# Head norms by products with ones and roots on every partition, and a block inverse kept in one orientation

## What is computed

```
qkv_a = causal_dwconv_silu(pad_front(qkv_a), conv_w)
qa = l2_norm(qa.reshape(B_, Lp, H_A, DK_A)) * (DK_A ** -0.5)
ka = l2_norm(ka.reshape(B_, Lp, H_A, DK_A))
o_a = gated_delta_rule(qa, ka, va, beta, g)[:, PAD:]
o_a = rms_norm_2(o_a, o_norm_a) * jax.nn.silu(z_a.reshape(B_, L, H_A, DV_A))
qb = rms_norm_2(qb.reshape(B_, L, H_B, DH_B), q_norm_b)
kb = rms_norm_2(kb.reshape(B_, L, H_B, DH_B), k_norm_b)
o_b = forgetting_attention(pad_front(qb), pad_front(kb), pad_front(vb), pad_front(log_f))[:, PAD:]
gate = jax.nn.sigmoid(gates.reshape(B_, L, 2, D_MODEL))
return jnp.sum(gate * y, axis=2) @ w_out
```

## Time and profile before

| | us |
|---|---|
| median of 3 runs | 1982.2 |
| lowest and highest run | 1977.0, 1984.1 |
| profiled execution, its time | 1981.22 |
| profiled execution, its span | 1979.9 |

### The profile page before, as it was taken

One profiled execution on the slowest core, in us unless ns is written; L12 is line 12 of the kernel. 1 busy time (PEld: TensorE's weight loads), 2 busy tenths in 40 slices (PEclk: granted clock), 3 DMA queues, 4 the chain that ended last, 5 costly groups with the idle time before them and its releaser, 6 DMA issues. The chain is left out here.

```text
span 1979.9 us, 23713 instructions
## 1 busy us (share of the span) xinstructions
PE 1785.5 (90%) x9424; PEld 1353.9 (68%) x9424; DVE 1232.4 (62%) x2155; ACT 718.6 (36%) x1243; POOL 434.1 (22%) x373
## 2 busy tenths in 40 slices
PE   7989999999999999998989999997878787887878
PEld 6869988977799879888979777893333333333333
DVE  4766655665576557654464445688776677667754
ACT  3545534344355346642342344343221122212211
POOL 0330000310000000004022000033555545454541
PEclk9989999999999999989989979998889988888889
DMA  6334555444445543412221211479999999999995
GB/s 261 110 114 149 191 183 180 170 153 166 165 176 190 182 177 110 149 64 80 92 68 62 86 62 67 170 287 421 422 421 421 422 422 421 422 422 421 421 422 245
DMA packets 62621, 453.76 MB, mean 229 GB/s; under 512 B 6944, under 2 KB 7072, under 8 KB 7856
## 3 DMA queue, kind: packets, MB, share of 16 engines
q0 software_dynamic: 36864, 268.45, 32.6%
q1 hardware_dynamic: 25040, 178.27, 25.4%
q10 hardware_dynamic: 608, 5.53, 0.7%
HBM read 451.18 MB, written 1.05 MB: 228 GB/s over the span
## 5 line engine op out<-in xcount | busy, mean ns | idle before, releaser
L2346 PE MATMUL banks<-uv_rows,diag 128*128 128x512 f32 x1024 | 509.8, 662 | 126.9 <-ACT diag L2395 122.5
L553 DVE TENSOR_TENSOR weights_lo<-weights,weights_hi 128x1024 fp32r<-128x1024 f32 x336 | 422.7, 1299 | 284.9 <-ACT weights_hi L544 282.3
L2346 PEld LDWEIGHTS banks<-uv_rows,diag 128*128 128x128 f32 x1024 | 215.4, 214 | 420.6 <-issue 269.3
L544 ACT ACTIVATE weights_hi<-weights 128x1024 fp32r<-128x1024 f32 x336 | 336.7, 1051 | 388.5 <-PE banks L560 380.2
L558 PE MATMUL banks<-x_hi,weights_hi 128*128 128x256 f32 (+1 forms) x1472 | 428.6, 291 | 6.7 <-DVE weights_lo L553 3.6
L560 PE MATMUL banks<-x_hi,weights_lo 128*128 128x256 f32 (+1 forms) x1472 | 422.0, 287 | 0.0
L559 PE MATMUL banks<-x_lo,weights_hi 128*128 128x256 f32 (+1 forms) x1472 | 421.8, 287 | 0.0
L2482 DVE CUSTOM_DVE_ANT_0 uv_rows<-uv_rows,tokens 128x1024 f32<-128x1024 f32 x256 | 306.4, 1224 | 165.1 <-DMA uv_rows<-expert_uv,index 165.0
L2505 POOL DMA_INDIRECT uv_rows<-expert_uv,index x256 | 310.9, 1214 | 339.9 <-PE banks L2346 285.5
L558 PEld LDWEIGHTS banks<-x_hi,weights_hi 128*128 128x128 f32 x1472 | 283.9, 193 | 16.8 <-issue 8.2
L560 PEld LDWEIGHTS banks<-x_hi,weights_lo 128*128 128x128 f32 x1472 | 283.6, 193 | 0.0
(11 more groups left out here) (379 smaller groups left out, 2239.8 us busy)
## 6 DMA issues: line engine op xcount, KB each, us to landing
weights<-weights SPq DMA_DIRECT2D x168, 1024.0 KB, 4.8
uv_rows<-expert_uv,index POOLq DMA_INDIRECT x256, 18.5
sb_first<-constants_first ACTq DMA_DIRECT2D x1, 1920.0 KB, 8.6
sb_always<-constants_always ACTq DMA_DIRECT2D x1, 1659.0 KB, 15.1
sb_peer<-constants_peer ACTq DMA_DIRECT2D x1, 1544.0 KB, 6.5
h<-x SPq DMA_DIRECT2D x1, 1024.0 KB, 5.7
out<-h SPq DMA_DIRECT2D x4, 256.0 KB, 4.7
sb_now<-constants_now ACTq DMA_DIRECT2D x1, 216.0 KB, 4.7
```

Of the source, the lines that this page charges most:

```text
L544: self.act.activation(self.w_hi[b % SLOTS][:, f], self.raw[b % SLOTS][:, f], ACT.Copy).then_inc(self.hi_made, 1)
L553: self.dve.tensor_tensor(self.w_lo[b % SLOTS][:, f], self.raw[b % SLOTS][:, f], self.w_hi[b % SLOTS][:, f], ALU.subtract).then_inc(self.lo ...
L2346: mm = pe.matmul(self.bank(2 * t + half), self.diag[:, k, :], self.uv[n % NUV][:, f], start=(u < NT and k == 0), stop=(u >= UNITS - NT and ...
```

## The change

- **Sums.** A product with an all-ones 128 by 128 matrix gives the sum of squares on every partition at once, two heads at a time (`tensor_sums`). ScalarE then takes Ln, with epsilon as its bias and the mean's factor as its scale, from the banks into the place of the squares, and Exp there (`scalar_roots`). VectorE multiplies with what stands there. `to_row` and the products with `pick` in `conv` and `outs` are gone (`pick` is still used for the rows G, beta and eG at the start of each group and in `forgetting`).
- **Order of the norms.** In `outs` queries and keys come first and the delta rule's output last. Fills stand between the sums. The forgetting attention starts when ScalarE has read all sums and VectorE has scaled queries and keys.
- **Second gates.** ScalarE moves them out of the bank as they are, and takes their sigmoid over 2048 columns at the start of `merge`, on which VectorE waits there.
- **Inverse.** Only `dTT` is kept. In each level TensorE first transposes it into a bank, and ScalarE copies this to `dT` beside its copy to `dM`. The product with `dB` and the one with `dM` work on the second half of each block's columns, 64 of 128, and VectorE subtracts there. In the last level the wide tiles multiply 64 by 64 quarters without a mask. Level 0 is made by VectorE for all tiles, in two operations, and the first masked block waits for `dA` alone.

```diff
-    c["to_row"] = np.broadcast_to(np.eye(H2).reshape(1, -1), (P, H2 * H2))
+    c["eps"] = np.full((P, 1), EPS)
...
+    def tensor_sums(self, squares, c, width):
+
+        for j in range(2):
+            mm = self.pe.matmul(self.bank(2 * (c % 3) + j, width), self.C["ones"][:, :], squares[:, j, :], start=True, stop=True)
+        mm.then_inc(self.rms_sums.sem, 1)
+
+    def scalar_roots(self, stage, squares, c, width, scale):
+        act = self.act
+        act.wait_ge(self.rms_sums.sem, self.rms_sums.at(stage, c + 1))
+        act.activation(squares, self.banks(2 * (c % 3), 2, width), ACT.Ln, bias=self.C["eps"][:, 0:1], scale=scale).then_inc(self.rms_read.sem, 1)
+        act.wait_ge(self.rms_read.sem, self.rms_read.at(stage, c + 1))
+        act.activation(squares, squares, ACT.Exp, scale=-0.5).then_inc(self.rms_ready.sem, 1)
...
         for c in range(8):
-            pe.wait_ge(self.rms_ready.sem, self.rms_ready.at("conv", c // 4 + 1))
+            pe.wait_ge(self.rms_sq.sem, self.rms_sq.at("conv", c + 1))
             if c < 3:
                 pe.wait_ge(self.freed_a.sem, self.freed_a.at("conv", st.n - 2 + c))
             else:
-                pe.wait_ge(self.rms_scaled.sem, self.rms_scaled.at("conv", c - 2))
...
+                pe.wait_ge(self.rms_read.sem, self.rms_read.at("conv", c - 2))
+            self.tensor_sums(self.conv_squares(c), c, SM)
+            if c in (2, 5, 7):
+                self.tensor_fill(CONV_FILLS[c // 3])
+        pe.wait_ge(self.rms_read.sem, self.rms_read.at("conv", 8))
...
+        act.preload_act_table_set(LN_EXP)
+        for c in range(8):
+            self.scalar_roots("conv", self.conv_squares(c), c, SM, 1.0)
+            if c in (2, 5):
+                self.scalar_fill(CONV_FILLS[c // 3])
         self.scalar_conv_silu(st.n - 1)
...
-            act.activation(self.y[c // KD][:, c % KD, :], self.bank(FILL_BANK, S), ACT.Sigmoid).then_inc(self.fill_moved, 1)
+            act.activation(self.y[c // KD][:, c % KD, :], self.bank(FILL_BANK, S), ACT.Copy if c // KD else ACT.Sigmoid).then_inc(self.fill_moved, 1)
...
-        wait("T0", 2)
-        wait("T0_pool", 1)
+        wait("A", 3)
         for lvl in range(1, 7):
             for t in self.active(lvl):
...
                 for hh in range(HG):
-                    mm = pe.matmul(ps[:, hh * n:(hh + 1) * n], b[:, hh, :], tt[:, hh, :], start=True, stop=True)
+                    if self.whole(lvl, t):
+                        pe.transpose(turned[0:half, hh * half:(hh + 1) * half], tt[0:half, hh, 0:half], C["ident"][0:half, 0:half])
+                    else:
+                        pe.transpose(turned[:, hh * n:(hh + 1) * n], tt[:, hh, :], C["ident"][0:n, 0:n])
+                if not self.whole(lvl, t):
+                    wait("B", i)
+                for hh in range(HG):
+                    if self.whole(lvl, t):
+                        mm = pe.matmul(ps[0:half, hh, 0, :], a[half:P, hh, 0:half], tt[half:P, hh, half:P], start=True, stop=True)
+                    else:
+                        mm = pe.matmul(ps[:, hh], b[:, hh, :], self.second(tt, lvl)[:, hh], start=True, stop=True)
...
-                act.activation(self.of("dM", t), self.level_bank(t, 0)[:, 0:HG * n].rearrange("p (h n) -> p h n", h=HG),
+                act.activation(self.of("dM", t)[0:rows, :, 0:n // 2],
+                               self.level_bank(t, 0)[0:rows, 0:HG * n // 2].rearrange("p (h n) -> p h n", h=HG), ACT.Copy)
+                act.activation(self.of("dT", t)[0:rows, :, 0:cols],
+                               self.level_bank(t, 1)[0:rows, 0:HG * cols].rearrange("p (h n) -> p h n", h=HG),
                                ACT.Copy).then_inc(d["M1"].sem, 1)
...
+            wait("masked", t + 1)
+            step.of(dve.tensor_tensor(self.of("dTT", t), at, self.each("next", n), ALU.mult))
             dve.wait_ge(step.sem, step.n)
+            dve.tensor_tensor(self.of("dTT", t), self.each("ident", n), self.of("dTT", t), ALU.subtract).then_inc(d["T0"].sem, 1)
...
-                if not final:
-                    step.of(dve.tensor_tensor(tm, tm, pz[:, 0:HG * n].rearrange("p (h n) -> p h n", h=HG), ALU.subtract))
-                    dve.wait_ge(step.sem, step.n)
-                dve.tensor_tensor(tt, tt, pzt[:, 0:HG * n].rearrange("p (h n) -> p h n", h=HG), ALU.subtract).then_inc(d["T"].sem, 1)
+                dve.tensor_tensor(tt, tt, pzt, ALU.subtract).then_inc(d["T"].sem, 1)
...
+    OUT_FILLS = {1: 41, 3: 42, 5: 43, 7: 44, 9: 45, 10: 46, 11: 47}
...
+        self.tensor_fill(BETWEEN_FILLS[0])
         pe.wait_ge(self.fa_v_put, 6)
         for c in range(12):
+            pe.wait_ge(self.rms_sq.sem, self.rms_sq.at("outs", 1 if c < 4 else 2))
             if c >= 3:
+                pe.wait_ge(self.rms_read.sem, self.rms_read.at("outs", c - 2))
+            self.tensor_sums(self.out_squares(c)[0], c, self.out_squares(c)[1])
+            if c in self.OUT_FILLS:
+                self.tensor_fill(self.OUT_FILLS[c])
...
+        act.activation(self.y[1][:, :, :], self.y[1][:, :, :], ACT.Sigmoid).then_inc(self.gates_b, 1)
```

## The result

The changed kernel takes 1926.6 us (median of four runs, 1924.6 to 1929.9) against 1981.5 of the kernel before, measured beside it. The ratio is 0.973, with a 95% interval of 0.970 to 0.975: it is faster, by 55 us. 1911 was forecast, so some 15 us of the expected gain are missing. The time lies inside the range, at the place that one of the rivals had named: *Loads bind*, 1925.

A forecast was written before the change was run, and what follows sets the result against it. TensorE was taken to bound the kernel before the experts; gains of 7.5 + 4.0 + 18.6 + 19.3 + 21.4 = 70.8 us off 1981.2 gave 1910.4, with the median's 1.0 1911.4, stated as 1911. Range 1895 to 1932.

The forecast's parts named there:

- Loads bind: Rival: in the levels, 320 records of 64 columns cost 0.112 us each, 17.0 us more; 1925 us, chance 0.12.
- The shift is lost: Rival: the experts start at the same time because weights don't arrive sooner; 1982 us, chance 0.02.
- The slow side: Rival: new short waits pull TensorE's clock to 1.2 GHz in tail, levels and norms, and it stays; 2045 us, chance 0.03.
- Not as it says: Rival: the first masked block still waits because GpSimd's queue is late; 6.9 + 6.3 us stay, 1924 us, chance 0.04.
- The price of a level product: Both groups' levels: a record of 64 moving columns costs 0.059 us against 0.112 for 128; gain 28.5 us with fewer products.
- the new waits: In the levels, TensorE waits for ScalarE's two copies per tile: 3.0 us in group 0, 3.3 in group 1.
- the load rule: The Trainium skill's weight load: columns over 1.2 GHz, 107 ns for 128 columns, so 64 moving columns save nothing in levels 1 to 5.
- The waits ahead of the levels: The first masked block needs only ScalarE's copy of A, so the stall goes: gain 6.3 us in group 0, 6.9 in group 1.
- The convolution: Convolution stage: dropping two sets of eight `to_row` products gains 7.5 us, and its end another 4.0.
- the tail: End of the convolution, up to the delta rule's first product: 23.0 us before, 19.0 after, gain 4.0.
- The norms: Norms after the delta rule: 61.9 us before, 40.5 after, gain 21.4; ends 37.9 and 48.
- ScalarE sets the pace: Rival: roots at 1.5 us and late level copies cost 8 in norms, 2 in tail, 6 in levels; 1927 us, chance 0.17.

The follow-up runs named there:

- forms2: Changed kernel with series of twelve unused products or transpositions, each behind sixteen full products; eight-row records took 0.115 us as products, 0.069 as transpositions.
- before_tall: Kernel before with all its picks, the norms' too, made over 128 rows with zeros, nothing else changed: 1955.9 us, ratio 0.987.
- rows128: Changed kernel with the rows of beta, G, eG and ncum on 128 partitions, zeros below the eighth, products over 128 rows: 1910.7 us, ratio 0.963.

## Why the prediction was right, and where it was off

**The bound and the direction** were right: TensorE is the engine to relieve, and what it was relieved of moved the experts' start from 1344.1 to 1290.1 us, with nothing given back behind it (635.8 and 633.2 us). *The shift is lost* and *The slow side* did not come true, nor did *Not as it says*. That the total fell within the range is in part luck. Of the 56.6 us between the profiles 3.5 lie ahead of the mixer and 2.6 in the experts, where nothing was changed; the norms gave 3.4 more than forecast, and the front of group 1 1.5 more, all of that the clock. These made up for a part of what the levels and the front of group 0 lack.

**The price of a level product** was wrong, and it is the step that failed: "I take 0.059; the ends are 0.057 and 0.112". The row behind it was of transpositions, and I noted against it only its eight rows. forms2 shows that the rows are innocent, and that the operation isn't: 0.069 for the transposition of eight rows, 0.115 for the product. The 320 records at 0.112 instead of 0.059 are 17.0 us. The prediction's own sign of it came: products of 64 columns are 2 x 0.105 = 0.21 us apart, where it had 0.22 for the loads and 0.118 for the forecast. The levels lack 29.9 - 17.1 = 12.8 us, and this divides so. The idle time in the levels fell by 3.3 us (5.2 to 1.9), where the forecast let it grow by 2.2: 5.5 better, because the new waits, priced at 6.3, hardly came; that slower products leave ScalarE more time is the likely reason and was not tested. The clock gave back 2.1 us instead of 3.7: 1.6 worse. What is left, 11.7 instead of 28.4, are the products: 16.7 worse. The rival *Loads bind* had this with a chance of 0.12, and the load rule stood beside it; it deserved the larger share, because a rule on products stood against a row on something else.

**The waits ahead of the levels** went as forecast: 3.7 and 3.9 us of idleness, against 4.1 and 3.9. **The clock** at the same place was mispriced. At the heads of the groups I saw the low clock only behind the wait for GpSimd and put it down to the wait ("the clock fell after 4 us of wait"). In group 1 it did go with the wait: the levels lost 2.4 us to it and now lose 0.1. But the eight-row products at the head of each group lower it on their own, and the kernel before had lost only 1.6 us to it in this execution, against 6.1 after: the 4.5 us that the front of group 0 lacks. That picks of eight rows and a clock of 0.66 stood together in the earlier trace rows was seen and not followed: with the remaining eight-row products counted as a cost, the forecast would have had a term for them.

**The convolution** was right, 12.3 against 11.5, and so were its parts: the span from the mixer to the first sums fell by 7.6 (7.5 forecast), the tail from 23.0 to 18.4 (19.0 forecast). The forecast of the tail priced every product at full clock and so held the clock's return without naming it; before_tall shows that it is all of that gain. **The norms** gained more, 24.8 against 21.4. ScalarE's pair of roots, here of the tail, is the reason that *ScalarE sets the pace* did not come true:

```profile
826.46 0.71 ACT L1536 ACTIVATE conv_sq<-banks,sb_always 128x544 f32<-128x544 f32 x1
827.20 0.66 ACT L1538 ACTIVATE conv_sq<-conv_sq 128x544 f32<-128x544 f32 x1
827.77 0.70 ACT L1536 ACTIVATE conv_sq<-banks,sb_always 128x544 f32<-128x544 f32 x1
```

A pair takes 827.77 - 826.46 = 1.31 us (forecast 1.25, the rival 1.5). TensorE is idle for 0.5 us in the whole stage: its own sum of 37.9 was the answer, and the wait for `branch_lo` comes later, 1.6 us in the forgetting stage, where I had counted it in the norms.

**Behind the norms** nothing was forecast and 5.5 us are lost. The 3.5 in the forgetting and merge stage belong to the new norms: with eight-row products that stage takes 122.3 to 124.2 us in the four profiles that have them and 119.0 and 119.1 in the two that don't. Idle time is 6.5 to 6.7 us against 4.7 and 4.9, of which 1.6 is that wait; the clock costs 5.8 to 7.8 against 4.0 and 4.3. The 2.0 in the queries stage are not told apart from what differs between executions: it lasts 51.6 to 53.6 us in ten profiles in which its code is the same. The same goes for the 3.5 us gained ahead of the mixer, where no instruction was changed: that point is reached between 730.1 and 735.7 us in the ten.

**The change beside its own side effect.** Part of the gain was the clock that the picks had cost. With tall products on both sides, in one comparison, the kernel before takes 1955.9 us and the kernel after 1910.7: the change itself is worth 45 us, the tall products some 26 us without it and 14 to 16 on top of it (13 to 18 by the ratios).

## What to carry to other kernels

Price a float32 product by the larger of its stationary and its moving columns, and take the price from a row of the same operation: a transposition's row says nothing of a product's load. Halving one of two sides of 128 brings nothing; leaving out whole products does. Where a program has products over a few rows and the granted clock is low behind them, give them 128 rows with zeros: it costs one clearing of the memory and no time on TensorE, and was worth 14 to 26 us here.

## What the runs showed of the hardware

- A float32 product record costs 0.110 to 0.118 us with 128 stationary columns, whether 8, 64 or 128 columns move and whether it has 8, 64 or 128 rows; 0.060 to 0.066 with 64 stationary columns and up to 64 moving. A transposition with 128 stationary columns costs 0.069 (8 rows), 0.071 (16), 0.075 (64) and 0.11 (128 rows, where 128 columns move).
- TensorE's clock went from 1.00 to 0.5 (1.2 GHz, against 2.4) behind 2.1 us of products with eight rows and 272 moving columns, without a wait (after), and stayed at 1.00 behind the same products over 128 rows (rows128). It also fell in forms2 at the end of series with eight moving columns (24 records, 2.8 us), once with eight rows and once with 128.
- How much the low clock costs at one place of one program differs by some 3 us between executions: the levels of group 0 lost 3.2 us in one execution of rows128 and 0.0 in the other.
